# Software-pipelining the experts of a two-layer diffusion backbone: the down product and spread of earlier experts between gate and up

## The reference, cut to what matters

```python
def ec_moe(h, w_router, w_gate, w_up, w_down):
    cap = EC_CAPACITY * n // N_EXPERTS            # 64 tokens for each expert
    aff = softmax(h @ w_router, over the tokens)
    g, idx = lax.top_k(aff, cap)
    xs = h[idx]                                   # 16 x 64 x 1024
    a = xs @ w_gate                               # w_gate, w_up, w_down: 16 x 1024 x 1024 each
    u = xs @ w_up
    y = (silu(a) * u) @ w_down * g
    return zeros.at[idx].add(y)                   # each expert's rows go back to their tokens
```

## Time and profile before

| | us |
|---|---|
| median of three runs | 1582.35 |
| lowest and highest | 1581.72, 1582.91 |
| span of the profiled execution | 1580.0 |
| experts of layer 0: first gate matmul to last down product weighed | 430.4 to 876.3 |
| experts of layer 1: the same | 1124.3 to 1570.5 |

### The profile page before, as it was taken

One profiled execution on the slowest core, in us unless ns is written; L12 is line 12 of the kernel. 1 busy time (PEld: TensorE's weight loads), 2 busy tenths in 40 slices (PEclk: granted clock), 3 DMA queues, 4 the chain that ended last, 5 costly groups with the idle time before them and its releaser, 6 DMA issues.

```text
span 1580.0 us, 16054 instructions
## 1 busy us (share of the span) xinstructions
PE 1458.4 (92%) x6698; PEld 680.3 (43%) x6698; DVE 670.3 (42%) x1152; ACT 229.7 (15%) x416; POOL 80.4 (5%) x72
## 2 busy tenths in 40 slices
PE   7999999999599999998889899999599999989997
PEld 4555655554233333333323688854233333333332
DVE  2577877434612232323222778725323232321223
ACT  2134344323200000000000200013000000000000
POOL 0010010000000000000000042000100000000000
PEclk9999999999799999999999999999799999999999
DMA  9962311695499999999999912553699999999996
GB/s 323 373 207 91 107 64 44 252 389 238 166 406 426 428 426 428 425 428 427 426 428 425 366 54 107 201 192 129 252 428 426 428 425 427 427 426 428 427 428 289
DMA packets 68593, 504.96 MB, mean 320 GB/s; under 512 B 8127, under 2 KB 18590, under 8 KB 39850
## 3 DMA queue, kind: packets, MB, share of 16 engines
q1 hardware_dynamic: 64618, 490.83, 76.1%
q0 software_dynamic: 2752, 8.92, 1.5%
q10 hardware_dynamic: 1152, 4.19, 0.7%
HBM read 497.62 MB, written 6.29 MB: 319 GB/s over the span
## 4 chain that ended last, share of the span: by engine, by line
PE 72%; DMA 18%; DVE 6%; ACT 2%; issue 1%; SPq 0%; DVEq 0%; POOLq 0%; ACTq 0%
PE ps L1106 31%; DMA work<-in_exp_w_up_dram 11%; PE ps L1190 9%; PE ps L965 7%; DMA ring<-in_exp_w_up_dram 6%; PE ps L1122 5%; PE ps L872 3%; PE ps L831 2%; PE ps L663 2%; PE ps L776 2%; PE ps L772 2%; PE ps L835 1%; PE ps L858 1%; PE ps L1144 1%; PE ps L1090 1%
## 5 line engine op out<-in xcount | busy, mean ns | idle before, releaser
L1106 PE MATMUL ps<-ring,work 128*64 128x512 f32 x1824 | 410.4, 599 | 30.1 <-ACT work L1471 13.1
L1106 PE MATMUL ps<-work 128*64 128x512 f32 x1248 | 281.9, 600 | 20.3 <-ACT work L1471 8.9
L2057 DVE TENSOR_TENSOR work<-ps,work 128x1024 f32<-128x1024 f32 x120 | 141.4, 1220 | 283.0 <-PE ps L1122 283.0
L1106 PEld LDWEIGHTS ps<-ring,work 128*64 128x64 f32 x1824 | 128.2, 138 | 293.6 <-issue 252.5
L1106 PEld LDWEIGHTS ps<-work 128*64 128x64 f32 x1248 | 87.3, 138 | 201.1 <-issue 171.4
L1122 PE MATMUL ps<-work 64*128 64x512 f32 x480 | 119.2, 615 | 0.0
L2075 DVE SCALAR_TENSOR_TENSOR work<-ps,gate_e,gate_ffn 128x512 f32<-128x512 f32 x32 | 24.0, 751 | 185.8 <-PE ps L1106 185.8
L2068 DVE TENSOR_TENSOR work<-work,ps 128x512 f32<-128x512 f32 x32 | 22.0, 688 | 173.6 <-issue 151.4
L1467 ACT ACTIVATE work<-ps 128x512 f32<-128x512 f32 x32 | 19.1, 597 | 487.3 <-PE ps L1106 487.3
L2245 POOL DMA_INDIRECT work<-xn_rows,row_no x32 | 30.6, 956 | 1037.9 <-PE ps L1090 733.3
L1471 ACT ACTIVATE work<-ps 128x512 f32<-128x512 f32 x32 | 19.1, 597 | 372.4 <-PE ps L1144 372.4
(11 more groups left out here) (324 smaller groups left out, 1371.0 us busy)
## 6 DMA issues: line engine op xcount, KB each, us to landing
ring<-in_exp_w_gate_dram SPq DMA_DIRECT2D x38, 2048.0 KB, 33.0
ring<-in_exp_w_up_dram SPq DMA_DIRECT2D x37, 2048.0 KB, 30.7
ring<-in_exp_w_down_dram SPq DMA_DIRECT2D x37, 2048.0 KB, 34.3
work<-in_exp_w_up_dram SPq DMA_DIRECT2D x27, 2048.0 KB, 30.4
work<-in_exp_w_gate_dram SPq DMA_DIRECT2D x24, 2048.0 KB, 35.0
work<-in_exp_w_down_dram SPq DMA_DIRECT2D x23, 2048.0 KB, 37.3
ring<-in_ada_w_dram SPq DMA_DIRECT2D x34, 1024.0 KB, 7.3
ring<-in_ada_w_dram SPq DMA_DIRECT2D x4, 2048.0 KB, 7.5
```

What stands on the lines that cost most here:

```text
L1106: last = mm(PS[64 * h:64 * h + 64, bank, :], lhsT[:, m * P + 64 * j:m * P + 64 * j + 64], slot_rows[sl][:, m, h * BANK:(h + 1) * BANK], st ...
L2057: v.tensor_tensor(row, PS[:, b:b + 2, :], row, ALU.add).then_inc(added[L], 1)
```

## The change: what it does, and the diff

The experts of a layer become a pipeline. The down product of expert e-1 stands behind the up product of expert e, and the spread of expert e-2 stands around that up product, where the spread of expert e-1 stood. The turning of `hid` for expert e comes after the down product of e-1, so that its copy `hidT` is needed only one expert later. The chunk numbers follow this new order of use: gate 0, up 0, gate 1, up 1, down 0, gate 2, up 2, down 1, and so on to gate 15, up 15, down 14, down 15. The ring and its rule stay, and so do the number and shape of all products. VectorE's order follows. After the last expert's hidden rows are turned, both halves of expert 14's spread and both chunks of expert 15's down product remain; they alternate. Chunk 95 is loaded in two halves, with a semaphore `last_in` for the first.

```diff
+        def gate_at(e):
+            return max(6 * e - 2, 0)
+        def up_at(e):
+            return gate_at(e) + 2
+        def down_at(e):
+            return min(6 * e + 8, CHUNKS - 2)
...
+                elif n == CHUNKS - 1:
+                    sp.dma_start(dst[:, 0:2, :], src[:, 0:2, :]).then_inc(last_in, 16)
+                    sp.dma_start(dst[:, 2:4, :], src[:, 2:4, :]).then_inc(slot_in[slot_of(L, n)], 16)
...
-                    halves(0, xsT[:, e % 2, :], 6 * e)
-                    if e >= 1:
-                        spread_rows(e - 1, 0)
+                        pe.wait_ge(silu_ok[L], e)
+                    halves(0, xsT[:, e % 2, :], gate_at(e))
+                    if e >= 2:
+                        spread_rows(e - 2, 0)
+                    if e >= 1:
                         pe.wait_ge(hid_ok[L], e)
-                    halves(1, xsT[:, e % 2, :], 6 * e + 2)
+                    halves(1, xsT[:, e % 2, :], up_at(e))
                     if e < E - 1:
                         rows_T(e + 1)
+                    if e >= 2:
+                        spread_rows(e - 2, 1)
                     if e >= 1:
-                        spread_rows(e - 1, 1)
+                        if e < E - 1:
+                            pe.wait_ge(xs_mod[L], e + 3)
                         pe.wait_ge(hidT_ok[L], e)
-                    pe.wait_ge(hid_ok[L], e + 1)
-                    for q in range(4):
-                        last = tr(PS[:, 3, q * P:(q + 1) * P], quarter(hid, q), ident)
-                    last.then_inc(hid_T[L], 1)
-                    pe.wait_ge(hidT_ok[L], e + 1)
-                    if e < E - 1:
-                        pe.wait_ge(xs_mod[L], e + 3)
-                    halves(2, hidT, 6 * e + 4)
+                        halves(2, hidT, down_at(e - 1))
+                    turn_hid(e)
+                spread_rows(E - 2, 0)
+                pe.wait_ge(hidT_ok[L], E)
+                for j in range(2):
+                    half_product(2, hidT, down_at(E - 1), j)
+                    if j == 0:
+                        spread_rows(E - 2, 1)
...
+                def weigh_rows(e):
+                    dve.wait_ge(used[L], down_at(e) + 2)
+                    v.scalar_tensor_tensor(out=y_s, in0=PS[:, 2, :], scalar=gate_e[:, e:e + 1],
+                                           in1=gate_ffn, op0=ALU.mult, op1=ALU.mult).then_inc(y_ok[L], 1)
...
                 for e in range(E):
-                    if e >= 1:
-                        add_rows(e - 1, 0)
+                    if e >= 2:
+                        add_rows(e - 2, 0)
...
+                    if e >= 2:
+                        add_rows(e - 2, 1)
                     if e >= 1:
-                        add_rows(e - 1, 1)
-                        pick_rows(e)
...
+                        pick_rows(e - 1)
+                        weigh_rows(e - 1)
+                add_rows(E - 2, 0)
+                add_rows(E - 2, 1)
+                pick_rows(E - 1)
+                weigh_rows(E - 1)
```

More of the change, by code:

```diff
@@ L178, in build, with matrix_of @@
         SPLIT = [SLOTS, SLOTS + 1, SLOTS + 2]
+        def gate_at(e):
[4 more added lines that the diff above has]
+            return min(6 * e + 8, CHUNKS - 2)
+        def matrix_of(n):
+            for e in range(E):
+                for kind, first in enumerate((gate_at(e), up_at(e), down_at(e))):
+                    if first <= n < first + 2:
+                        return kind, e, n - first
         def slot_of(L, n):
@@ L481, in load_chunk @@
             def load_chunk(L, n):
[L482 removed]
+                kind, e, half = matrix_of(n)
                 dst = slot_rows[slot_of(L, n)]
[L484 removed]
+                src = (exp_w_gate, exp_w_up, exp_w_down)[kind][L, e][half * HALF:(half + 1) * HALF, :].rearrange("(p m) n -> p m n", m=4)
                 if n in SPLIT:
@@ L1091, in rows_T, with half_product @@
                     last.then_inc(xs_T[L], 1)
+                def half_product(bank, lhsT, n0, j):
+                    n = n0 + j
+                    sl = slot_of(L, n)
+                    for m in range(4):
+                        if n == 0 and m % 2 == 0:
+                            pe.wait_ge(xs_mod[L], m // 2 + 1)
+                        if m == 0 and n in SPLIT:
+                            pe.wait_ge(half_in[n - SLOTS], 16 * (L + 1))
+                        elif m == 0 and n == CHUNKS - 1:
+                            pe.wait_ge(last_in, 16 * (L + 1))
+                        elif m == 0 or m == 2 and (n in SPLIT or n == CHUNKS - 1):
+                            pe.wait_ge(slot_in[sl], 16 * loads_of(L, n))
+                        for h in range(2):
+                            last = mm(PS[64 * h:64 * h + 64, bank, :], lhsT[:, m * P + 64 * j:m * P + 64 * j + 64],
+                                      slot_rows[sl][:, m, h * BANK:(h + 1) * BANK],
+                                      start=j == 0 and m == 0, stop=j == 1 and m == 3)
+                        if m == 1 and n < len(SPLIT):
+                            last.then_inc(half_used[L], 1)
+                    last.then_inc(used[L], 1)
@@ L1111, in halves @@
-                        last.then_inc(used[L], 1)
+                        half_product(bank, lhsT, n0, j)
                 def spread_rows(e, r):
@@ L1124, in spread_rows, with turn_hid @@
                     last.then_inc(spread[L], 1)
+                def turn_hid(e):
+                    pe.wait_ge(hid_ok[L], e + 1)
+                    if e >= 1:
+                        pe.wait_ge(hidT_ok[L], e)
+                    for q in range(4):
+                        last = tr(PS[:, 3, q * P:(q + 1) * P], quarter(hid, q), ident)
+                    last.then_inc(hid_T[L], 1)
                 rows_T(0)
@@ L1463, in experts @@
                 for e in range(E):
-                    act.wait_ge(used[L], 6 * e + 2)
+                    act.wait_ge(used[L], gate_at(e) + 2)
                     if e >= 1:
@@ L1469, in experts @@
                     if e >= 1:
-                        act.wait_ge(used[L], 6 * e)
+                        act.wait_ge(used[L], down_at(e - 1) + 2)
                     f(hidT, PS[:, 3, :], ACT.Copy).then_inc(hidT_ok[L], 1)
```

31 lines of the change are left out of this document (4 added, 27 removed).

## The result

| | before | after |
|---|---|---|
| median of five runs beside each other, us | 1582.35 | 1588.42 |
| lowest and highest | 1581.61, 1582.91 | 1587.89, 1589.07 |
| ratio, 95% interval | | 1.0037, 1.0027 to 1.0048 |
| span of the profiled execution | 1580.0 | 1586.3 |

The change costs 6.1 us, where the forecast had 3.1; the time lies above its range of 1578.0 to 1587.6. The two spans differ by 6.3 us, and can be compared stage by stage.

A forecast was written before the change was run, and what follows sets the result against it. The prediction took the weights' stream at 427 GB/s as the bound; other terms cost 0 and each layer's longer end 1.53 us, so 1582.35 + 3.1 = 1585.4 us, range 1578.0 to 1587.6.

The forecast's parts named there:

- The stream bounds the experts: In both layers' experts, weights arrive at a fixed 427 GB/s, 29.5 us an expert, whatever TensorE does.
- the 22 us: TensorE's idle waits for the hidT copy, 32 x 0.69 us, are removed but gain nothing, covered by the weights' stream.
- Rival 2: In the experts, the stream is not the bound and the 22 us come out: 1560 us; chance 0.03.
- The tail: Each layer's end, from chunk 93's product to the last weighing: 15.60 us against 14.07, 1.53 us more.
- rival 3: Only one layer pays; a wait at the convolution's start absorbs layer 0's delay of 1.5 us: 1583.9 us; chance 0.13.
- The halving: At each layer's end, loading chunk 95 in two halves gains 0, as it lands before TensorE reaches it.
- Rival 1: A layer's end hangs on chunk 95's landing and the halving pays, -2.2 us a layer: 1578.0 us; chance 0.12.
- The new wait at expert 1: At expert 1, with no spread yet, TensorE waits 1.5 us for modulate, taken from the lead at no cost.
- All later stages move rigidly: From the convolution on, layer 0's delay passes through unchanged, at no further cost.
- rival 4: The clock falls in the work behind chunk 93, costing 1.8 us more: 1587.2 us; chance 0.08.

The follow-up runs named there:

- fewer-bytes pair: Kernel before and changed kernel, each fetching only three of four rows of each ring chunk: 1553.56 us and 1542.19 us.
- old_end_both: Changed kernel with the last expert back in the order of before (down 14 ahead of up 15) in both layers: 1582.32 us, ratio 1.0005.
- early_fill: early_spread plus three unused matmuls in TensorE's idle times ahead of the convolution: 1581.32 us, ratio 0.9995 against before.
- before_fewer: Kernel before with only three of four rows of each ring chunk fetched, all products still made: 1553.56 us, ratio 0.9820.
- early_spread: Kernel before with expert 14's half spreads behind expert 15's first and second gate chunks and chunk 95 loaded in halves: 1581.78 us, ratio 0.9996.

## Why the prediction was right, and where it failed

**The stream bounds the experts, and the 22 us are worth nothing: right.** 427 GB/s before and after; 4.8 us of waiting for the copy gone in seven experts and 6.5 us of waiting for weights come. Per expert (29.5 of the 200 us) that is 1.8 us of waiting for weights before and 2.7 after; I had 2.6 and 3.3, both too high, with the rise of about the right size. The fewer-bytes pair is the counter-test: once the stream does not bind, the same edit is worth 12.9 us. Rival 2 falls with the unchanged 427 GB/s and the unchanged time of old_end_both.

**The tail: right, and exact.** 15.60 us forecast, 15.63 measured in all twelve layer ends with the new order at full bytes; +1.56 a layer against +1.53. Putting the old end back took the loss away in either layer. Both layers pay, so rival 3 is out: the convolution began 10.42 us after the weighing as before, and the 1.88 us of idle time took up nothing.

**The halving: right at nothing.** No wait before chunk 95 with or without it. Rival 1 asked for TensorE to be at chunk 95 within 10.0 us of chunk 93; it got there after 11.93 us (1572.40 - 1560.47).

**The new wait at expert 1: right.** Forecast 1.5 us, hidden by the lead. TensorE, layer 1 after:

```profile
1163.85 3.65 PE L1130 MATMUL ps<-ring,work 128*64 128x512 f32 x16 [1.51 <-DVE work L2083]
```

From expert 2 on no wait for `modulate` is among TensorE's waits.

**What failed: "All later stages move rigidly", and the place of rival 4.** The prediction let layer 0's delay pass through the convolution at no further cost. It costs 2.5 to 2.6 us there when the clock falls. 1.5 us are the fall itself, because TensorE's products set the pace behind it and no stream hides them. 1.0 to 1.1 us are a wait for VectorE that comes only when VectorE, late by the tail and the fall together, meets GpSimd's run; the prediction had no term for that. Rival 4 had the right mechanism and a price of 1.8 us, near the 1.5 here and the 1.7 in early_fill, but it looked only behind chunk 93, where waits for DMA had been seen to end in a fall, and it got 0.08. The fall came one stage later, at idle times that wait for VectorE, which stood in the earlier trace rows (1.88 us) and were cited there for another rival.

Of the traces with layer 0's end late and those idle times left open, five of seven show the fall; of those with the early end, none of five at full bytes (before_fewer, early and with fewer bytes, does); of those with the idle times filled, none of three. The times of many runs say the same. Take from each median what it stands above before on its chip, and from that the tails or the added work by the trace: 0.9 to 3.0 us are left in the seven runs with the late end and open idle times, and -0.7 to 0.5 in five of the others at full bytes. early_spread and early_fill do not fit: with 0.94 us a layer for their shorter ends, their medians stand 1.7 and 1.0 us too high. So the later end raises the chance of the fall; it does not fix it. Why a shift of 1.1 to 1.9 us raises it, these runs do not tell: the idle times themselves are the same to 0.02 us.

The Trainium skill (TensorE: Matmul & The Clock Gate, A second HAM failure mode) tells of a kernel whose TensorE stood idle for short moments between groups of products often enough that its clock went back and forth. The trace agrees as to kind: two gaps of 1.05 and 1.88 us about a short group of transposes, and a clock of 0.59 behind them, though here it is one fall and one return. By that rule the idle times ahead of the convolution should have been a rival of their own in the forecast.

**VectorE beside GpSimd: shown in every trace.** The seventeen traces have 816 instructions of the kind on line 2158 (the four of `weight_sums`, two SBUF inputs of 128x512) in the convolution. The 128 that began while GpSimd's run was under way took 1.64 to 1.76 us, and the other 688 took 0.68 to 0.70. Most of the 128 cost nothing, since TensorE does not wait for them.

**A smaller part stays open.** 3.12 for the tails and 2.3 for the convolution and router make 5.4 of the 6.3 us between the two spans. The rest lies in chunk 93's landing (0.36 and 0.30 us later) and in layer 0's start (0.27). Over all traces at full bytes, chunk 93's product starts 431.83 us after the layer's first product in the twelve layers with the new end (431.2 to 432.5) and 431.36 in the ten of the old order (430.7 to 432.2). The ranges overlap, but the means lie 0.47 us apart, nearly three times the standard error that the scatter of these layers gives (0.16). old_end_both shows nothing of it in its time. The pipelined order may bring chunk 93 some 0.5 us later; the cause, if it is more than scatter, stays open.

**The numbers.** The likeliest time was 3.0 us too low. The range ended at 1587.6, which the prediction does not work out; it had room for one fall of 1.8 us on top of a tail of 3.1, which is 1587.2. A stage that follows a shifted one and has idle times of its own should have widened it.

## What to carry to other kernels

Where a stream of weights sets the pace, a spared wait inside the loop is worth nothing, and a reordering is worth what it does to the work behind the last load that is waited for: count that first, and let the last pass keep the order with the least behind it, even if the loop is pipelined. A stage that starts later is not always only later: look for short idle times of TensorE at its start, since the clock can fall there in one kernel and not in the other, and for work of GpSimd that does not move along, since VectorE can come to stand beside it. Ask also what the edit would be worth with fewer bytes, since that tells a good edit that is covered from one that is no good.

## What the runs showed of the hardware

The granted clock differs from run to run of one and the same kernel at the same place. Behind the same idle times one run of the changed kernel went on at 1.00 and another at 0.64, with 1.97 and 3.59 us for the same product. Medians of one and the same kernel scatter more than its tails do: 1587.11 to 1588.42 for the changed kernel.

Idle time that costs nothing by itself can still have a price: in layer 0 the 1.86 us before expert 0's down product (the new wait at expert 1) end in a lower clock, which the lead then hides. TensorE and the window there, after:

```profile
465.28 5.35 PE L1130 MATMUL ps<-ring,work 128*64 128x512 f32 x16 [1.86 <-DVE work L2083]
```

and

```profile
466.00:470.00 4.00, 4.00 (x14) 1.26 (x12) 0.00 (x0) 0.00 (x0) 0.00 (x0) 0.64 1.03 426
```

Three matmuls without use, in time that was idle, brought the changed kernel to 3.65 us above before in place of 4.9 to 6.1, each on its own chip, and cost the kernel before nothing (0.9999).

A VectorE instruction with two SBUF inputs of 128x512 takes 0.69 us alone and 1.64 to 1.76 us when it begins while GpSimd works through element-wise instructions of the same size. How much that costs hangs on when the two meet.
